# Stick-breaking attention summed by parts: value differences, shifted by DMA, in place of a second sigmoid and a product

## The reference, cut to what matters

```python
def stick_breaking_attention(u, w_q, k, v, w_o):
    """o_t = sum_{s<t} beta_ts prod_{s<j<t}(1-beta_tj) v_s, beta = sigmoid(q.k/sqrt(d))."""
    ...
            z = jnp.einsum("bhqd,bhkd->bhqk", qi, kj).astype(jnp.float32)
            valid = jnp.logical_or(jnp.logical_not(is_diag), diag_mask)
            lo = jnp.where(valid, jax.nn.log_sigmoid(-z), 0.0)
            after = jnp.einsum("bhqj,js->bhqs", lo, later) + acc[..., None]
            logw = jnp.where(valid, z + lo + after, -jnp.inf)
            o = o + jnp.einsum("bhqk,bhkd->bhqd", jnp.exp(logw).astype(vj.dtype), vj)
```

## Time and profile before

| | |
|---|---|
| median of 3 executions | 2448.83 us (2448.54, 2448.83, 2456.0) |
| the profiled execution: time, span | 2456.86 us, 2455.1 us |
| TensorE busy, share of the span | 2375.3 us, 97% |
| VectorE, ScalarE, GpSimd busy | 42%, 25%, 59% |
| granted TensorE clock, mean | 0.986 |
| sb_project and sb_attend | 835 to 967 us and 967 to 1057 us of the span |

### The profile page before, as it was taken

One profiled execution on the slowest core, in us unless ns is written; L12 is line 12 of the kernel. 1 busy time (PEld: TensorE's weight loads), 2 busy tenths in 40 slices (PEclk: granted clock), 3 DMA queues, 4 the chain that ended last, 5 costly groups with the idle time before them and its releaser, 6 DMA issues.

```text
span 2455.1 us, 34580 instructions
## 1 busy us (share of the span) xinstructions
PE 2375.3 (97%) x14346; PEld 1935.6 (79%) x14346; DVE 1021.6 (42%) x1558; ACT 609.9 (25%) x1271; POOL 1458.5 (59%) x1260
## 2 busy tenths in 40 slices
PE   8999999999999999999999999999798999999998
PEld 6887778888888886678888877766686788888887
DVE  3547673551141502954305264885532325211114
ACT  2223663020010112721102022356442211110010
POOL 7665777586586665029759647650123766665863
PEclk9999999999999999999999999999898999999999
DMA  5331114232232232014323313120001332332321
GB/s 168 92 89 44 52 52 153 80 120 95 86 112 95 80 109 78 1 44 137 101 71 121 96 54 103 52 86 10 3 4 36 99 97 83 104 101 79 108 89 62
DMA packets 104432, 199.04 MB, mean 81 GB/s; under 512 B 9322, under 2 KB 12628, under 8 KB 104276
## 3 DMA queue, kind: packets, MB, share of 16 engines
q1 hardware_dynamic: 101620, 189.36, 24.9%
q10 hardware_dynamic: 2656, 7.47, 0.9%
HBM read 194.71 MB, written 2.10 MB: 80 GB/s over the span
## 4 chain that ended last, share of the span: by engine, by line
PE 73%; DVE 6%; POOL 3%; issue 1%; ACT 1%; DVEq 0%; POOLq 0%; ACTq 0%
PE psum L160 32%; PE psum L304 25%; PE psum L162 4%; PE psum L242 3%; POOL weight_split_ring L446 2%; DVE big L1591 1%; PE psum L204 1%; DVE big L2058 1%; POOL weight_split_ring L443 1%; PE psum L1513 1%; DVE best L2057 1%; PE psum L2370 0%; PE psum L1541 0%; PE psum L2299 0%; PE psum L2363 0%
## 5 line engine op out<-in xcount | busy, mean ns | idle before, releaser
L446 POOL TENSOR_TENSOR weight_split_ring<-weight_ring,weight_split_ring 128x512 fp32r<-128x512 f32 (+3 forms) x732 | 962.1, 1335 | 30.5
L160 PE MATMUL psum<-x_split,weight_split_ring 128*128 128x512 f32 x4128 | 970.7, 393 | 4.0 <-POOL weight_split_ring L446 2.4
L160 PEld LDWEIGHTS psum<-x_split,weight_split_ring 128*128 128x128 f32 x4128 | 766.4, 187 | 176.0 <-issue 10.5
L443 POOL TENSOR_SCALAR weight_split_ring<-weight_ring 128x1024 fp32r<-128x1024 f32 (+3 forms) x366 | 395.3, 1080 | 675.1 <-PE psum L304 369.8
L304 PE MATMUL psum<-weight_split_ring,hidden_split 128*128 128x512 f32 x2256 | 514.1, 389 | 0.0
L304 PEld LDWEIGHTS psum<-weight_split_ring,hidden_split 128*128 128x128 f32 x2256 | 423.0, 188 | 87.5
L162 PE MATMUL psum<-weight_split_ring,x_split 128*128 128x512 f32 x864 | 217.8, 400 | 0.3 <-ACT big L1872 0.3
L162 PEld LDWEIGHTS psum<-weight_split_ring,x_split 128*128 128x128 f32 x864 | 156.4, 188 | 37.8 <-issue 7.2
L762 DVE TENSOR_TENSOR big<-big 128x512 f32<-128x512 f32 x64 | 88.0, 1375 | 177.2 <-ACT big L747 177.2
L747 ACT ACTIVATE big<-psum 128x512 f32<-128x512 f32 x64 | 38.3, 599 | 429.7 <-PE psum L160 374.9
L545 DVE SCALAR_TENSOR_TENSOR residual<-residual,psum 128x512 f32<-128x512 f32 x48 | 32.7, 682 | 218.1 <-PE psum L304 217.9
(11 more groups left out here) (352 smaller groups left out, 2440.8 us busy)
## 6 DMA issues: line engine op xcount, KB each, us to landing
weight_ring<-in_mlp_w SPq DMA_DIRECT2D x128, 512.0 KB, 3.7
weight_ring<-in_w_in SPq DMA_DIRECT2D x92, 512.0 KB, 3.6
weight_ring<-in_w_ffn_in SPq DMA_DIRECT2D x40, 512.0 KB, 3.7
weight_ring<-in_w_out SPq DMA_DIRECT2D x24, 512.0 KB, 3.7
weight_ring<-in_w_ffn_out SPq DMA_DIRECT2D x22, 512.0 KB, 3.6
weight_ring<-in_sb_w_q SPq DMA_DIRECT2D x8, 512.0 KB, 3.8
weight_ring<-in_sb_w_k SPq DMA_DIRECT2D x8, 512.0 KB, 3.7
weight_ring<-in_sb_w_v SPq DMA_DIRECT2D x8, 512.0 KB, 3.6
```

The costliest lines, as they stand in the source:

```text
L160: mm = pe.matmul(out, wp[:, k, m * P:m * P + rows], xp, start=first, stop=last)
L443: pool.tensor_scalar(part.high[:, 0:nk, 0:n], raw, 1.0, 0.0, ALU.mult, ALU.add).then_inc(self.high_made, 1)
L446: low = pool.tensor_tensor(part.low[:, k, 0:n], raw[:, k, :], part.high[:, k, 0:n].bitcast(F32), ALU.subtract)
```

## The change

The second sigmoid and the product with it go. keep, after the scan, is the survival S and is transposed itself. The output products take value differences instead of values. For that each value tile is copied one token further into a new tile vStep by DMA from SBUF to SBUF (127 rows within the block, and the last row to the first of the next block), issued by ScalarE behind its copy; VectorE then subtracts vTok from vStep, giving the differences, and writes into vTok the differences with the last row of the block made to end the sum there. The diagonal block of a unit is multiplied with vTok, the blocks before it with vStep. Steps 0 to 3 (the first half of the width) are done in sb_project, steps 4 to 7 in sb_attend, one behind each scan of units 4 to 7. The output products wait for the steps of their half. The logits wait for the one sigmoid that is left. wT moves to the tile of the gain rows, since vStep takes its place.

```diff
@@ sb_project
+    s_vs = [kit.sem(f"sb_shifted_values_landed{n}") for n in range(2)]
+    m.sb_steps = kit.sem("sb_value_steps_ready")
+    def cols(n):
+        return slice(n // NT * WIDE, (n // NT + 1) * WIDE)
+    def value_step(dve, n):
+        v, d = m.vTok[:, n % NT, cols(n)], m.vStep[:, n % NT, cols(n)]
+        dve.wait_ge(s_vs[n // NT], 16 * (2 * NT - 1))
+        kit.vector_chain(dve)(dve.tensor_tensor(d, d, v, ALU.subtract))
+        dve.scalar_tensor_tensor(out=v, in0=v, scalar=m.ident[:, P - 1:P], in1=d, op0=ALU.mult, op1=ALU.add)\
+           .then_inc(m.sb_steps, 1)
...
         for n in range(gv.count):
             ps = gv.wait_tile(act, n)
-            act.activation(m.vTok[:, n % NT, (n // NT) * WIDE:(n // NT + 1) * WIDE], ps, ACT.Copy)\
-               .then_inc(kit.tile_free, 1)
+            b = n % NT
+            act.activation(m.vTok[:, b, cols(n)], ps, ACT.Copy).then_inc(kit.tile_free, 1)
+            gv.wait_free(act, n)
+            act.dma_start(m.vStep[1:P, b, cols(n)], m.vTok[0:P - 1, b, cols(n)]).then_inc(s_vs[n // NT], 16)
+            if b < NT - 1:
+                act.dma_start(m.vStep[0:1, b + 1, cols(n)], m.vTok[P - 1:P, b, cols(n)]).then_inc(s_vs[n // NT], 16)
+
+    def vector(dve):
+        kit.vector_chain(dve)(dve.memset(m.vStep[0:1, 0, :], 0.0))
+        for n in range(NT):
+            value_step(dve, n)
...
@@ sb_attend, tensor
-                pe.wait_ge(s_b, u - 1)
+                pe.wait_ge(s_k, u - 1)
...
-                    mm = pe.transpose(kit.psum[:, TURNED + s, block(b)], weights(u)[:, s, block(b)], m.ident[:, :])
+                    mm = pe.transpose(kit.psum[:, TURNED + s, block(b)], keep(u)[:, s, block(b)], m.ident[:, :])
...
+            pe.wait_ge(m.sb_steps, NT if p < PAIRS // 2 else 2 * NT)
             for b in range(i + 1):
+                v = m.vTok if b == i else m.vStep
                 for s in range(2):
                     h = 2 * p + s
-                    mm = pe.matmul(kit.psum[rows(s), OUT + p % 2, block(i)], m.vTok[:, b, h * 64:(h + 1) * 64],
+                    mm = pe.matmul(kit.psum[rows(s), OUT + p % 2, block(i)], v[:, b, h * 64:(h + 1) * 64],
                                    turned(u)[:, s, block(b)], start=(b == 0), stop=(b == i), skip_group_check=True)
@@ sb_attend, scalar
             act.activation(keep(u), logit_banks(u), ACT.Sigmoid, scale=-1.0).then_inc(s_k, 1)
-            act.activation(weights(u), logit_banks(u), ACT.Sigmoid).then_inc(s_b, 1)
@@ sb_attend, vector
-                step.mark(dve.tensor_tensor_scan(x, x, m.ones[:, 0:1].broadcast_to([P, n]), 1.0, ALU.mult, ALU.mult))
-            step.wait()
-            dve.wait_ge(s_b, u + 1)
-            w = weights(u)[:, :, 0:n - 1]
-            dve.tensor_tensor(w, w, keep(u)[:, :, 1:n], ALU.mult).then_inc(s_w, 1)
+                ins = dve.tensor_tensor_scan(x, x, m.ones[:, 0:1].broadcast_to([P, n]), 1.0, ALU.mult, ALU.mult)
+            ins.then_inc(s_w, 1)
...
         for u in range(U + 4):
             if u < U:
-                breaks(u)
+                survive(u)
+            if NT <= u < 2 * NT:
+                m.sb_value_step(dve, u)
             if u >= 7 and u % NT == 3:
                 low(u // NT - 1)
@@ Memory
-        self.keep, self.broken = self.part(b, 12288, 3, 2, SEQ), self.part(b, 15360, 3, 2, SEQ)
-        self.wT = self.part(b, 18432, 2, 2, SEQ)
+        self.keep = self.part(b, 12288, 3, 2, SEQ)
+        self.vStep = self.part(b, 16384, NT, D)
+        self.wT = self.part(r, 0, 2, 2, SEQ)
```

More of the change, by code:

```diff
@@ L1453, in scalar @@
             ps = gv.wait_tile(act, n)
-            act.activation(m.vTok[:, n % NT, (n // NT) * WIDE:(n // NT + 1) * WIDE], ps, ACT.Copy)\
-               .then_inc(kit.tile_free, 1)
+            b = n % NT
[8 more added lines that the diff above has]
+            value_step(dve, n)
     def gpsimd(pool):
         kit.split_chunks(pool, gv.last_chunk + SPLIT)
-    return tensor, None, scalar, gpsimd
+    m.sb_value_step = value_step
+    return tensor, vector, scalar, gpsimd
 def sb_attend(nc, kit, m, a):
@@ L1471, in sb_attend @@
     s_k = kit.sem("sb_keep_ready")
[L1472 to L1475, removed]
+    s_w = kit.sem("sb_survival_ready")
+    s_t = kit.sem("sb_survival_transposed")
+    s_c = kit.sem("sb_survival_copied")
     s_o = kit.sem("sb_out_ready")
@@ L1498, in keep @@
         return m.keep[:, u % 3, :, 0:width(u)]
-    def weights(u):
-        return m.broken[:, u % 3, :, 0:width(u)]
     def turned(u):
@@ L1582, in vector, with survive @@
     def vector(dve):
-        step = kit.vector_chain(dve)
-        def breaks(u):
+        def survive(u):
             dve.wait_ge(s_k, u + 1)
```

## The result

The changed kernel is slower: 2497.01 us median of four executions (2495.39 to 2498.87) against 2452.41 us for the kernel before (2448.54 to 2459.1), a ratio of 1.018 with a 95% interval of 1.0164 to 1.0195. The forecast was 2441.6 us with a range up to 2450. The profiled executions differ by 38.5 us (2495.39 to 2456.86).

The account below looks back on a forecast made before the run. TensorE bounds most of the span, but VectorE's product was taken to set the attention's pace. Gains of 1.03, 5.7 and 0.46 us, other terms at 0, sum to 7.2: 2448.83 - 7.2 = 2441.6 us, range 2438 to 2450.

Parts of the forecast that it names:

- Added in the projection: ScalarE's 14 shift DMAs behind its value copies: issues of 0.60 us, landing in 3 to 6 us, all hidden.
- Rival (d): Projection: shift DMAs land late and hold the meeting, from a 19 us landing on; 2458.6 us at 36 us; chance 0.08.
- The product held the pace: Attention: VectorE's product delays TensorE's transposes; without it a pair of heads takes 9.64 us against 10.78, 1.14 less.
- ScalarE "was not full": Attention: ScalarE loses four sigmoids, some 2.8 us a pair of heads, but was not full.
- The wait ahead of each O block: TensorE, attention: one more wait before each of 32 output blocks, taken as 0, at most 3.5 us.
- Value steps, 1.35 us and covered with nothing over: VectorE, first attention pair: steps 4 to 7 take 1.35 us each, 5.4 in all, just covered by TensorE's work.
- T8: TensorE's transposes of unit 8 in the attention: forecast to start near 993.55 us instead of 994.58, 1.03 us earlier.
- What the prediction said on contention: Projection: value steps 0 to 3 meet about two GpSimd weight splits, delaying them some 2 us each; 0 in the sum.
- The sum of 7.2 us: Attention phase: total gain forecast from the start of T8, the five pairs after it and the end.
- 5.7 + 0.46 = 6.16: Attention from T8 on: five pairs of heads at 1.14 us give 5.7, a shorter wait at the end 0.46.
- Rival (c): TensorE's clock behind the meeting: a denser stream leaves 1.2 GHz earlier, 2 to 3 us more off, 2439 us; chance 0.10.
- Carrying the difference of one execution over: Whole kernel: the profiled 2456.86 us lies 8.0 over the median 2448.83, so the gain was subtracted from the median.

Follow-up runs that it names:

- grouped run: Changed kernel with the shift in three DMAs per half (112, 15 and 1 rows) instead of seven, same result: 2449.25 us, ratio 0.9978 to the kernel before.
- small DMAs later: The grouped run with the second half's two small DMAs issued behind the attention's first sigmoid: 2447.81 us, ratio 0.9964 to the kernel before.
- no shift: Changed kernel without any shift DMA, vStep zeroed instead, value steps kept: 2447.57 us, ratio 0.9967 to the kernel before.

## Why the prediction was wrong

**The step that failed** is "Added in the projection": "Issue: one took 0.60 us on this queue, the longest there", from it "So ScalarE is hidden even then", and "I take 3 to 6 us" for the landing. The price came from DMAs of 64 or 128 rows and was used for 127. The transfer takes 10.1 us, not at most 5.9, and what I treated as a fixed cost of issuing contains the wait for room: 4.8 to 13.6 us instead of 0.60. Measured where the sum has nothing for the DMAs: 47.6 us at the meeting and about 3 us more at step 4 (86.2 us for the phase against 83.4 without DMAs). With 126 rows the large issues took 0.77 to 0.82 us behind the first (0.60 predicted at most), and the meeting moved by half a microsecond.

While weights were loading, a tile took longer still. The first half landed at 990.6 us, where 948 was forecast: four tiles in 53.2 us from the first issue at 937.4, or 13.3 us each, and the other four by 1031.5, 10.2 us each. That the weights on the same engines make the difference was not tried.

**Rival (d)** had the right place, the shift DMAs, and the right sign, with a chance of 0.08, but half of the mechanism. It asked for a landing of over 19 us and held against it the bytes. The landings were 18 us (issued at 972.5 and landed at 990.6, issued at 1013.0 and landed at 1031.5), under its bound; but the first half's last DMA was issued at 972.5 and not by 942, since ScalarE stood behind its own issues. Steps 0 to 3 ended at 996.3, so its path alone would have moved the meeting by some 30 us; ScalarE's copies and issues of the second half, in the same queue, held it until 1014. I had cited a page of the Trainium skill there for packets that are not too small; the section of the same page that bears on the row count I had left out. Eight transfers of 10.08 us from 937.4 us on cannot end before 1018 us, 51 us behind the meeting of the kernel before; that sum was open to me but for the 10.08.

**The product held the pace: right.** A pair took 10.78 us with it put back alone, 9.71 to 9.72 without. I had forecast 9.64. The 0.07 us are not explained.

**ScalarE "was not full": half right.** With the sigmoid alone put back a pair takes 10.14 us. Removing only the product would have gained 0.6 of the 1.07 us; busy shares did not show that, since the copy behind the sigmoid is what TensorE waits for.

**The wait ahead of each O block, taken at 0: right.** The step from T of six to O of sixteen takes 0.81 us with the wait added, where it took 0.80:

```profile
1074.96 0.64 PEld L1549 LDWEIGHTS psum<-constants,big 128*128 128x128 f32 x6 [0.16 <-DVE big L1610]
1075.77 0.85 PEld L1563 LDWEIGHTS psum<-gain_rows,big 128*64 128x64 f32 x16 [0.17 <-issue]
```

**Value steps, 1.35 us and covered with nothing over: right.** In the grouped run step 4 takes 1.37 us (from 982.67 to the next scan at 984.04), T8 waits 0.1 us or less. What the prediction said on contention held as well: the steps of the first half meet GpSimd's subtractions and stretch, from 0.69 and 0.75 us up to 1.77 and 1.66. They are over before the last split, which takes its 2.48 us as before:

```profile
951.52 0.69 DVE L1450 TENSOR_TENSOR big<-big 128x512 f32<-128x512 f32 x1 [108.16 <-DMA big<-big]
952.25 0.75 DVE L1451 SCALAR_TENSOR_TENSOR big<-big,constants 128x512 f32<-128x512 f32 x1
...
954.98 1.77 DVE L1450 TENSOR_TENSOR big<-big 128x512 f32<-128x512 f32 x1
956.79 1.66 DVE L1451 SCALAR_TENSOR_TENSOR big<-big,constants 128x512 f32<-128x512 f32 x1
```

**The sum of 7.2 us: right for the attention, in part by luck.** The phase was forecast at 90.7 - 7.2 = 83.5 us; five versions whose DMAs are quick or absent took 82.4 to 83.5 us (grouped 83.0, small DMAs later 83.3, no shift 83.4). Their medians are 6 to 9 us under the kernel before that was measured beside them. By terms, from T8 on the gain was 5.85 us in each of the five (56.9 us to mix2 against 62.76), where 5.7 + 0.46 = 6.16 had been forecast. Up to T8 it was 1.3 to 2.5 us, where 1.03 had been. The two misses cancel in part.

**Rival (c)**, an earlier rise of TensorE's clock, came true in a small part and goes with the spread up to T8. Over the first 20 us from the first logits the granted clock was 0.74 on average in the kernel before, and 0.76, 0.77, 0.78, 0.79 and 0.83 in the five versions, with phases of 83.5, 83.4, 83.3, 83.0 and 82.4 us: the earlier the clock rose, the shorter the phase. These are single executions, so how much of it the change brings is not shown.

**Carrying the difference of one execution over: wrong by 6.6 us.** The 27 executions of the kernel before beside the first experiments go from 2448.53 to 2461.22 with a median of 2455.47. So 2448.83 was at the low end, and the profiled 2456.86, called 8.0 us too long, was an ordinary one. That is why the versions that gain what was forecast, or more, still lie near 2448 us and not at 2441.6, and it is probably why two of the first forecasts (126 rows, grouped) came out 1 and 3 us low. From the first product of mix2 to the end, the same code took from 1392.9 to 1399.0 us in the traces.

## What to carry to other kernels

Before a DMA is called cheap, look at its number of rows and not only at its bytes: with 127 and with 113 rows, both prime, these ran on a single engine, and splitting off a few rows (127 as 112 and 15) made the shift quick. A DMA issue shares its queue with the work of the engine that issues it, so when transfers back up, the engine's own instructions stop; read the issues' durations and ask what stands behind them. A base of three executions can be off by more than the gain that is forecast. And a thing taken off the bounding engine pays only up to the next bound, which an experiment that puts one removed thing back shows better than busy shares do.

## What the runs showed of the hardware

- One DMA engine moved 25.8 GB/s from SBUF to SBUF (127 rows of 2 KB in 10.08 us), with a DMA share of 0.07. 122 rows went at 51 to 53 GB/s with a share of 0.14, 125 rows at 127 GB/s with 0.33. Tiles of 127 and 113 rows took 10.1 and 9.1 us, 122 rows 5.0 to 6.6, 125 and 126 no visible time.
- ScalarE's queue took about two of these transfers. After its last large issue had ended, the data landed 17.9 us later with 127 rows (1013.65 to 1031.5), that is 1.8 transfers; 16.6 us with 113 rows. The issues that had to wait took 4.8 to 13.6 us in the changed kernel, whether of 127 rows or of one.
- An issue costs by its shape too: 0.70 to 0.77 us for 112 rows in four blocks, 0.91 to 1.47 us for 15 rows in four blocks, 0.76 to 1.63 us for one row in three blocks, against 0.54 to 0.66 us for one row in one block.
- TensorE's granted clock was 0.50, that is 1.2 GHz, from 970 us to the end of the idle stretch and in the first 10 us of work after it: 0.50 on average from 1010 to 1020 us, 0.80 from 1020 to 1030 and 1.00 after, so it rose near 1024 us, with work since 1014. In the kernel before the same happened at the shorter meeting.
